# Hybrid attention and expert-retrieval step on one core: experts gathered by pairs of heads from within the query stage, inverse roots by ACT as exponentials of logarithms

## The chip, the cores and the metric

The kernel runs on one core of one Trainium2 chip. The metric is the device time of one execution in microseconds (us), the median of several runs. The engines are called by the names of the profile: PE (matrix engine), DVE (vector engine), ACT (activation engine), POOL (GpSimd, which issues the gathers and half of the cache pages here) and SP (which issues the other transfers). The core has 16 DMA engines.

## The reference, cut to what matters

One layer for 512 prompt tokens and 8 sample tokens, all in float32. Of the parts, these matter here:

```python
def rmsnorm(x, g):
    y = x * lax.rsqrt(jnp.mean(x * x, axis=-1, keepdims=True) + RMS_EPS)
    return y * g

xn = rmsnorm(h, norm1_g); z = xn @ w_in                      # "first" norm
qa = rmsnorm(qa, qa_norm_g); ka = rmsnorm(ka, ka_norm_g)     # "head" norms, 8 heads x 64
ya = sb_attend(qa, (past_k, ka), (past_v, va), ...)          # samples read 32 pages of 128 keys each
ob, s_new = gla_scan(...); yb = rmsnorm(ob, ob_norm_g) * silu(rb)   # "output" norm, 4 heads x 128
h = h + (ga * (ya @ w_up_a) + gb * (yb @ w_up_b)) @ w_o
h = h + peer(rmsnorm(h, norm2_g), w_peer_q, peer_sub_keys, expert_u, expert_v)
h = h + (p @ w_ple) * sigmoid(rmsnorm(h, norm3_g) @ w_ple_gate)

def peer(x, w_q, sub_keys, expert_u, expert_v):
    q = (x @ w_q).reshape(t, 8, 2, 128)                      # 8 heads, 2 halves
    s = einsum('thcd,hcnd->thcn', q, sub_keys)               # 128 scores for each of 16 lists
    s1, i1 = top_k(s[:, :, 0], 16); s2, i2 = top_k(s[:, :, 1], 16)
    top_s, top_c = top_k(s1[..., :, None] + s2[..., None, :], 16)    # per head, of 256 sums
    e = i1[top_c // 16] * 128 + i2[top_c % 16]               # 8 heads x 16 experts a token
    g = softmax(top_s)
    act = gelu(einsum('td,thkd->thk', x, expert_u[e]))
    return einsum('thk,thkd->td', g * act, expert_v[e])
```

Each token so reads 128 experts, and each expert is a row of 1024 values of u and 1024 of v (8 KB).

## The kernel before

The five engines run programs written out by hand; semaphores order them, and nothing reorders them. A single program goes through these stages:

- **Front.** The first norm, the projections (items of PE that ACT takes out of the banks), the head norms, the gated linear attention, and the output norm. For each norm PE makes the mean of squares, ACT its root (`roots`, `ob_root`), and DVE a reciprocal and the products (`head_norm`, `ob_norm`).
- **Samples' cache.** Eight samples read 32 pages of keys and 32 of values each (256 KB a page). POOL issues the key pages into `kring` (8 slots); DVE multiplies and sums them by pairs of pages (`keys`, one pair is one multiplication and one reduction), as filler between its other steps; `HEAD_KEYS` says how many pairs stand in each head of the attention stage. The value pages go into `vring` (8 slots): the first `V_EARLY * PAGES` are issued by SP, the others by POOL, and from sample 5 on they use `kring` too, once the last keys are multiplied. PE multiplies value pages in half rings of four pages (`v_half`), and each sample ends with `own_heads` on DVE, `v_fold` on PE and `take_v` on ACT.
- **Attention stage**, 8 heads; then the **gate stage** of pass 0 (tokens 0 to 255): `gate_tiles`, `up_tiles` on PE, `mix_rows` on DVE, 8 times; then `wo_tiles` (8 times), the second norm, the transposes.
- **Query stage** of pass 0: 16 times `queries(0, j)` and `scores(0, j - 1)` on PE, `take_queries` and `take_scores` on ACT, `key_lists(0, j)` on DVE (the best 16 of 128 scores, for two tiles of 128 tokens). After lists 4, 8, 12 and 15 DVE selects the experts of tile 0 for a pair of heads (`select_pair`), and `select_end` makes the 128 expert numbers and gates of each token at once. Value pages of samples 5 to 7 are multiplied between the queries (`V_IN_PQ`), and the folds stand at `FOLD_PQ`.
- **Gather stage**, 4 tiles of 128 tokens, 32 steps a tile, 128 steps in all. A step works on four of the eight slots of `gring`. POOL issues one indirect DMA for each slot (128 rows of 8 KB, line 654), DVE makes the dot products (line 1519), ACT the gelu, the coefficients and two diagonal matrices (lines 1049 to 1058), PE multiplies (`expert_values`, line 1984) and so frees two slots at a time (`g_used`). Odd slots use lists whose halves are swapped; SP copies these (`other_lists`). `second_pass` puts the whole of pass 1 (gates, wo, queries, 48 weight tiles of 512 KB) and the selection of tiles 1 and 2 between the steps of tiles 0 and 1; `embeddings` puts the final norm and the selection of tile 3 and of the samples between the steps of tiles 2 and 3.
- **Tail**: the last tile's sums, the samples' experts, the final norm and the outputs.

The gather stage waits for all value pages, since `gring` lies over the rings: POOL waits on `v_done` for 8 samples and on `y_taken`, and then on `sel_ready` and `lists_landed` for each tile, which are counted by tile. Weight tiles go through `wring` (3 slots) in the order of `stream` on SP; a tile waits there until PE has used the one three before it. Nearly every operation of DVE and ACT is recorded at line 154, that of the helper `also`, so groups are told apart by operation and size; `L1116` and `L1128` are the sum and the product of `keys`, `L1657` `v_half`, `L1850` and `L1862` gates and ups, `L1878` wo, `L1907` queries, `L1917` scores, `L1668` folds, `L623` pages issued by POOL.

## Time and profile before

| | us |
|---|---|
| median of 3 runs | 2206.96 (2206.49 to 2214.03) |
| the profiled execution | 2213.31 |
| its span, first to last instruction | 2211.6 |
| outside the span | 1.7 |

The page gives the busy time of each engine, the span in 40 slices, the DMA queues and the chain of work that ended last. To place the stages on the time axis, read three instructions: the last page issued by POOL, the first gather, and the last gather. The windows then show how many GB/s were moved in each stage, and the timelines of single engines show which of them was late. "Granted clock" (PEclk) is a share of the full 2.4 GHz. All times are those of the one profiled execution.

### The profile page before, as it was taken

The page shows a single profiled execution, that of the slowest core. Times are in us where ns is not written, and L with a number is a line of the kernel's source. Part 1 is how long each engine was busy: PE and PEld are TensorE (multiplying, and loading weights), DVE is VectorE, ACT ScalarE, POOL GpSimd, SP SyncE. Part 2 cuts the span into 40 slices and gives each one's busy share as a digit, 9 for nine tenths or more (in the row PEclk, how much of TensorE's full clock was granted, in tenths as well). Part 3 has the DMA queues.
Part 4 walks back from the last instruction along what each step waited for, and adds up shares of the span by engine and source line. Part 5 has one row for each costly group of instructions (what it writes and reads, how often), then busy time and mean ns, then how long its engine had stood idle before and what let it go on. Part 6 is the DMA issues. An engine that isn't in the chain of part 4 may idle for free.

```text
span 2211.6 us, 23735 instructions
## 1 busy us (share of the span) xinstructions
PE 1644.4 (74%) x8044; PEld 762.6 (34%) x8044; DVE 1396.0 (63%) x2571; ACT 618.7 (28%) x1772; POOL 792.8 (36%) x911
## 2 busy tenths in 40 slices
PE   7999976999899277776867886455758555765559
PEld 5638622558456133332213443111212111211112
DVE  2697679769438666565455789556766556666442
ACT  2212213531011134443232222223242223232221
POOL 1131123223353234333443344343444444444430
PEclk9999988999999689998988988777888877877779
DMA  4574497879797599999999999999999999999990
GB/s 149 186 269 169 150 367 252 293 272 343 283 332 295 198 420 419 420 420 391 408 398 420 419 414 391 420 417 397 419 421 412 418 421 413 422 421 421 391 421 18
DMA packets 150698, 769.20 MB, mean 348 GB/s; under 512 B 21544, under 2 KB 23048, under 8 KB 82736
## 3 DMA queue, kind: packets, MB, share of 16 engines
q0 software_dynamic: 105632, 645.98, 72.6%
q1 hardware_dynamic: 44944, 121.70, 15.2%
q8 instruction: 63, 1.03, 0.2%
q14 instruction: 59, 0.48, 0.1%
HBM read 759.41 MB, written 5.58 MB: 346 GB/s over the span
## 4 chain that ended last, share of the span: by engine, by line
DMA 41%; PE 34%; DVE 10%; issue 6%; ACT 4%; POOL 4%; SPq 1%; POOLq 0%; DVEq 0%; ACTq 0%
DMA arena<-experts_in,arena 38%; PE bank L1984 8%; PE bank L1575 5%; POOL arena L654 4%; DVE arena L154 4%; PE bank L1626 3%; DVE arena L1519 3%; PE bank L1657 2%; PE bank L1878 2%; PE bank L1907 2%; DMA arena<-cache_v_in 2%; PE bank L1967 2%; DVE arena L1116 2%; DVE arena L1128 2%; ACT arena L154 1%
## 5 line engine op out<-in xcount | busy, mean ns | idle before, releaser
L1984 PE MATMUL bank<-arena 64*64 64x512 f32 x4096 | 652.0, 768 | 487.6 <-ACT arena L1058 476.4
L1519 DVE CUSTOM_DVE_ANT_0 arena<-arena 128x1024 f32<-128x1024 f32 x512 | 622.6, 1227 | 534.4 <-DMA arena<-experts_in,arena 532.0
L654 POOL DMA_INDIRECT arena<-experts_in,arena x512 | 575.7, 1124 | 856.5 <-PE bank L1984 710.7
L1984 PEld LDWEIGHTS bank<-arena 64*64 64x64 f32 x4096 | 160.2, 160 | 938.7 <-ACT arena L1058 699.6
L1049 ACT ACTIVATE arena<-arena 128x2 f32<-128x2 f32 x256 | 52.1, 203 | 932.0 <-DVE arena L1519 931.8
L623 POOL DMA_DIRECT2D arena<-cache_k_in x256 | 137.8, 538 | 418.7 <-DVE arena L1128 346.9
L1128 DVE TENSOR_TENSOR arena<-arena 128x1024 f32<-128x1024 f32 x128 | 156.4, 1223 | 25.9 <-DMA arena<-scratch_q 14.1
L1116 DVE TENSOR_REDUCE arena<-arena 128x16 f32<-128x1024 f32 x128 | 155.0, 1214 | 0.0
L154 ACT ACTIVATE arena<-bank 128x512 f32<-128x512 f32 (+7 forms) x126 | 54.1, 441 | 308.8 <-PE bank L1575 115.5
L1907 PE MATMUL bank<-arena 128*128 128x256 f32 (+1 forms) x512 | 125.5, 398 | 0.8 <-ACT arena L154 0.8
L1575 PE MATMUL bank<-arena 128*128 128x260 f32 x512 | 122.0, 397 | 5.0 <-DVE arena L154 5.0
L1053 ACT ACTIVATE arena<-arena 128x1 f32<-128x1 f32 x512 | 122.8, 286 | 8.4
L1850 PE MATMUL bank<-arena 128*128 128x256 f32 (+1 forms) x512 | 120.9, 392 | 0.0
L154 DVE TENSOR_TENSOR arena<-arena 128x512 f32<-128x512 f32 (+6 forms) x131 | 108.4, 830 | 12.1 <-ACT arena L154 8.4
L154 ACT ACTIVATE arena<-bank,arena 128x512 f32<-128x512 f32 (+3 forms) x134 | 68.4, 551 | 158.7 <-PE bank L1850 73.0
L1907 PEld LDWEIGHTS bank<-arena 128*128 128x128 f32 x512 | 97.6, 196 | 39.6 <-issue 24.4
L1575 PEld LDWEIGHTS bank<-arena 128*128 128x128 f32 x512 | 99.4, 196 | 28.0 <-issue 11.2
L1850 PEld LDWEIGHTS bank<-arena 128*128 128x128 f32 x512 | 97.2, 193 | 33.4 <-issue 18.0
L1657 PE MATMUL bank<-arena 128*8 128x512 f32 x512 | 97.0, 616 | 14.8 <-DMA arena<-cache_v_in 14.7
L154 ACT ACTIVATE arena<-arena 128x260 f32<-128x260 f32 (+11 forms) x98 | 64.1, 677 | 138.4 <-DVE arena L154 84.7
L154 DVE TENSOR_TENSOR arena<-arena,bank 128x512 f32<-128x512 f32 (+3 forms) x74 | 39.3, 568 | 85.8 <-PE bank L1878 25.0
L623 POOL DMA_DIRECT2D arena<-cache_v_in x128 | 68.9, 538 | 68.1 <-PE bank L1657 46.2
(100 smaller groups left out, 1571.8 us busy)
## 6 DMA issues: line engine op xcount, KB each, us to landing
arena<-cache_k_in POOLq DMA_DIRECT2D x256, 256.0 KB, 5.0
arena<-w_stream_in SPq DMA_DIRECT2D x120, 512.0 KB, 6.5
arena<-cache_v_in SPq DMA_DIRECT2D x128, 256.0 KB, 5.9
arena<-cache_v_in POOLq DMA_DIRECT2D x128, 256.0 KB, 5.4
arena<-experts_in,arena POOLq DMA_INDIRECT x520, 12.6
arena<-xT_in SPq DMA_DIRECT2D x2, 1040.0 KB, 6.3
arena<-scratch_q SPq DMA_DIRECT2D x1, 2048.0 KB, 7.2
arena<-x_rows_in SPq DMA_DIRECT2D x2, 1024.0 KB
```

What stands on the lines that cost most here:

```text
L154: op(*args, **kw).then_inc(sem, 1)
L623: pool.dma_start(slot, cache[bass.ds(page, 1)].rearrange("a p n -> (a p) n")).then_inc(landed, 16)
L654: pool.indirect_dma_start(gring[:, s, :], None, A["experts"], bass.IndirectOffsetOnAxis(ap=rows[:, i * RING_G + s:i * RING_G + s + 1], axi ...
L1053: last = A_(coef[:, s:s + 1], gates_of[:, i * 8 + s:i * 8 + s + 1], ACT.Copy, scale=act_g[:, s:s + 1])
L1116: V.tensor_reduce(z4[:, b:b + 1, first:first + 2, :].rearrange("p a c h -> p (a c) h"), prod[:, 2 * (n % 2):2 * (n % 2) + 2].rearrange("p ...
L1128: V.tensor_tensor(prod[:, 2 * (n % 2):2 * (n % 2) + 2], kring[:, 2 * i:2 * i + 2], q, ALU.mult).then_inc(k_mul, 1)
L1519: last = V.tensor_tensor_reduce(gring[:, s, 0:D], gring[:, s, 0:D], x_rows, 1.0, 0.0, ALU.mult, ALU.add, dot[:, s:s + 1])
L1575: last = mm(out, w[:, k], xn[:, k, a:b], start=(k == 0), stop=(k == KD - 1))
L1657: mm(out[at:at + H, :], w4[:, b, PAGES - 1 - g * RING_V - s], slot, start=False, stop=True, skip_group_check=True).then_inc(v_free, 1)
L1850: last = mm(bank[4 + u][:, 0:b - a], w[:, k], xn[:, k, a:b], start=(k == 0), stop=(k == KD - 1))
L1907: last = mm(bank[4 + j % 2][:, 0:b - a], w[:, k], xn2T[p][:, k, 0:b - a], start=(k == 0), stop=(k == KD - 1))
L1984: last = mm(bank[2 * r + c2][out, :], diag[rows, s], gring[rows, s, cols], start=start, stop=True, skip_group_check=True)
```

## The change

**Pairs.** Tile by tile selection becomes selection by pairs of heads. `select_end` works on the 32 experts of a pair, and `softmax_exp`, `soft_in`, `soft_e`, `sel_ready`, `lists_landed` and `other_lists` are counted by pair (four to a tile); the samples keep theirs in one. POOL's gathers of slots 0, 32, 64 and 96 of a tile wait for their own pair.

**Query stage cut.** Ahead of the first gather stand only 10 of the 16 queries of pass 0, 7 of the 16 key lists and pair 0 of tile 0. The other queries, lists and pairs 1 to 3 go between steps 0 and 15 of the gather stage, and pass 1 begins at step 12 (`PASS_AT`), 12 steps later than before. Tables (`QUERIES_AT`, `LISTS_AT`, `PAIRS_AT`, `EMBED_AT`) give the step of each piece.

**Value pages earlier.** SP issues 160 pages in place of 128, the last 32 of them between weight tiles of the gate and wo stages. POOL issues 96, all into the ring of 16 slots. PE's half rings of samples 4 to 7 stand in the gates (4 of them), in wo (14, before 8) and in the first 7 queries (14, before 24). Six pairs of key pages move from the gate stage into the attention stage (`HEAD_KEYS` 36 in sum, before 30; gates 26, before 32).

**Inverse roots.** In the first, head and output norms ACT makes ln(mean + eps) and exp(-0.5 x), in place of a square root on ACT and a reciprocal on DVE. The second and final norms stay.

The memory of the gather stage is laid out in another order, so that the swapped rows (`xsw`) lie where the keys' queries were, and not in a ring.

```diff
-V_EARLY = 4
-V_WIDE = 5 * PAGES
+V_EARLY = 5
+V_FIRST = V_EARLY * PAGES
 V_BANK = (7, 0, 0, 0, 2, 0, 2, 0)
...
-V_IN_PQ = {0: (5, 0), 1: (5, 2), 2: (5, 4), 3: (5, 6), 4: (6, 0), 5: (6, 2), 6: (6, 4), 7: (6, 6),
-           8: (7, 0), 9: (7, 2), 10: (7, 4), 11: (7, 6)}
-V_AFTER = {2: 2, 3: 3, 5: 4, 6: 5, 7: 6}
...
-MASK_PQ = {3: 5, 7: 6, 11: 7}
-FOLD_PQ = {1: 4, 6: 5, 10: 6, 14: 7}
-HEAD_KEYS = (4, 4, 4, 4, 4, 4, 3, 3)
+HEAD_KEYS = (5, 5, 5, 5, 4, 4, 4, 4)
+GATE_KEYS = (4, 4, 3, 3, 3, 3, 3, 3)
+V_IN_GATES = {4: (4, 0), 5: (4, 1), 6: (4, 2), 7: (4, 3)}
+V_IN_WO = {0: ((4, 4),), 1: ((4, 5), (5, 0)), 2: ((4, 6), (5, 1)), 3: ((4, 7), (5, 2)), 4: ((5, 3), (5, 4)),
+           5: ((5, 5), (5, 6)), 6: ((5, 7), (6, 0)), 7: ((6, 1),)}
+V_IN_PQ = {0: (6, 2), 1: (6, 4), 2: (6, 6), 3: (7, 0), 4: (7, 2), 5: (7, 4), 6: (7, 6)}
...
+FIRST_QUERIES, FIRST_LISTS = 10, 7
+QUERIES_AT = ({-1: 9, 0: 10, 1: 11, 3: 12, 4: 13, 5: 14, 6: 15},
+              {g: j for j, g in enumerate((49, 50, 51, 52, 55, 56, 57, 58, 61, 62, 63, 64, 67, 68, 69, 70))})
+LISTS_AT = ({0: 7, 3: 8, 4: 9, 5: 10, 6: 11, 9: 12, 10: 13, 11: 14, 12: 15},
+            {g + 3: j for g, j in QUERIES_AT[1].items()})
+PAIRS_AT = {(0, 1): 1, (0, 2): 7, (0, 3): 13, (1, 0): 17, (1, 1): 23, (1, 2): 29, (1, 3): 35,
+            (2, 0): 56, (2, 1): 62, (2, 2): 68, (2, 3): 74, (3, 0): 78, (3, 1): 82, (3, 2): 86, (3, 3): 90}
+PASS_AT = 12
+EMBED_AT = (76, 92, 108)
+SAMPLE_LISTS_AT = 77
+PAIR_SLOTS = 32
...
-            ("gring", RING_G * 2 * D), ("diag", RING_G * HP), ("xsw", 2 * D), ("expert_sw", 2 * SEL), ("gate_sw", 2 * SEL)])
+            ("xsw", 2 * D), ("expert_sw", 2 * SEL), ("gate_sw", 2 * SEL), ("diag", RING_G * HP), ("gring", RING_G * 2 * D)])
...
+            for m in range(8):
+                stream(gate_use(0, m, 0) + RING_W, gate_use(0, m, 0) + 2 * RING_W)
...
+                elif m == 5:
+                    early_pages(4 * PAGES + RING_V, 4 * PAGES + 2 * RING_V)
+                elif m == 7:
+                    early_pages(4 * PAGES + 2 * RING_V, 4 * PAGES + 3 * RING_V)
+            stream(wo_use(0, 3), wo_use(0, 5))
+            early_pages(4 * PAGES + 3 * RING_V, 5 * PAGES)
+            stream(wo_use(0, 5), pq_use(0, 3))
...
-                sp.wait_ge(sel_ready, t + 1)
+            def other_lists(t, pair):
+                if t // 2 or pair:
+                    sp.wait_ge(lists_landed[t % 2], 64 * (4 * (t // 2) + pair))
+                sp.wait_ge(sel_ready, 4 * t + pair + 1)
+                slots = slice(PAIR_SLOTS * pair, PAIR_SLOTS * pair + PAIR_SLOTS)
                 for to, of in both_halves:
-                    sp.dma_start(expert_sw[to, t % 2], expert[of, t]).then_inc(lists_landed[t % 2], 16)
-                    sp.dma_start(gate_sw[to, t % 2], gate[of, t]).then_inc(lists_landed[t % 2], 16)
-
...
-            sp.wait_ge(v_done, NB)
-            sp.wait_ge(y_taken, 5)
+            sp.wait_ge(k_mul, K_PAIRS + NB * PAGES // 2)
             sp.wait_ge(xn2_ready, 2)
             other_rows(0)
             other_rows(1)
-            other_lists(0)
-
-
-            stream(gate_use(1, 1, 0), wo_use(1, RING_W))
-            other_lists(1)
+            stream(pq_use(0, 3), pq_use(0, 11))
...
-            for i in range(V_EARLY * PAGES // RING_V, NB * PAGES // RING_V):
+            for i in range(V_FIRST // RING_V, NB * PAGES // RING_V):
...
-                    if n < V_WIDE:
-                        pool.wait_ge(v_free, n + 1)
-                    elif n < V_WIDE + RING_K:
+                    if n < V_FIRST + RING_K:
                         pool.wait_ge(k_mul, K_PAIRS + NB * PAGES // 2)
+                    elif n < V_FIRST + 2 * RING_V:
+                        pool.wait_ge(v_free, RING_V + n - 2 * RING_V + 1)
                     else:
-                        pool.wait_ge(v_free, n - 2 * RING_V + RING_V + 1)
+                        pool.wait_ge(v_wide_free, n - V_FIRST - 2 * RING_V + 1)
                     load_page(slot, A["cache_v"], landed, pages[s])
...
-                pool.wait_ge(sel_ready, t + 1)
-                pool.wait_ge(lists_landed[t % 2], 64 * (t // 2 + 1))
                 for i in range(SEL // RING_G):
                     for s in range(RING_G):
+                        pair, slot = divmod(i * RING_G + s, PAIR_SLOTS)
+                        if slot == 0:
+                            pool.wait_ge(sel_ready, 4 * t + pair + 1)
+                        elif slot == 1:
+                            pool.wait_ge(lists_landed[t % 2], 64 * (4 * (t // 2) + pair + 1))
...
+            def inverse_root(out, mean, signal):
+                c.also(A_, out, mean, ACT.Ln, bias=cst("eps"))
+                c.then(A_, out, out, ACT.Exp, scale=-0.5, signal=signal)
+
...
-            c.also(V.reciprocal, rstd, std_row)
...
-                c.then(V.reciprocal, std, std)
...
-                c.then(V.reciprocal, ob_tmp[:, h % 3], ob_tmp[:, h % 3])
...
+            def softmax_exp(t, pair=0):
+                act.wait_ge(soft_in, 4 * t + pair + 1)
+                heads = slice(2 * pair, 2 * pair + 2) if t < NT else slice(0, PH)
+                c.also(A_, top[0:ROWS[t], 1, heads], top[0:ROWS[t], 1, heads], ACT.Exp, signal=soft_e)
...
+            def selection(g):
+
+                for (t, pair), at in PAIRS_AT.items():
+                    if g == at + 1:
+                        softmax_exp(t, pair)
...
+            def select_end(t, heads):
+
+                R, each = ROWS[t], heads.stop - heads.start
+                slots = slice(TOPK * heads.start, TOPK * heads.stop)
                 c.settle()
                 flat = lambda x: x.rearrange("p h k -> p (h k)")
-                c.also(V.scalar_tensor_tensor, out=expert[0:R, t], in0=flat(top[0:R, 7]), scalar=float(NKEYS), in1=flat(top[0:R, 8]),
-                       op0=ALU.mult, op1=ALU.add)
-                dve.wait_ge(soft_e, t + 1)
-                c.also(V.tensor_reduce, den[0:R], top[0:R, 1], AX.X, ALU.add)
-                c.then(V.reciprocal, den[0:R], den[0:R])
-                c.then(V.tensor_tensor, gate[0:R, t].rearrange("p (h k) -> p h k", h=PH), top[0:R, 1],
...
-            for j in range(16):
+            for j in range(4):
                 key_lists(0, j)
-                if j in MASK_PQ:
-                    own_heads(MASK_PQ[j])
-                if j in (4, 8, 12, 15):
-                    pair = (j - 3) // 4 if j < 15 else 3
-                    select_pair(0, pair, False)
-                    select_pair(0, pair, True)
+            select_pair(0, 0, False)
+            own_heads(6)
+            select_pair(0, 0, True)
+            for j in range(4, FIRST_LISTS):
+                key_lists(0, j)
+                if j == 4:
+                    own_heads(7)
...
+                if m in V_IN_GATES:
+                    v_half(*V_IN_GATES[m])
...
+                for b, half in V_IN_WO[i]:
+                    v_half(b, half)
-            for j in range(16):
+            for j in range(FIRST_QUERIES):
...
+                for p in range(2):
+                    if g in QUERIES_AT[p]:
+                        queries(p, QUERIES_AT[p][g])
+                    if g - 1 in QUERIES_AT[p]:
+                        scores(p, QUERIES_AT[p][g - 1])```

**Where instructions stand.** PE at the end of the query stage, before. `L1907` is a query, `L1917` scores, `L1668` a fold, `L1850` a gate tile of pass 1, `L1984` the products of gathered experts:

```order
L1907 MATMUL bank<-arena 128x256 x8
L1917 MATMUL bank<-arena 128x128 x2
L1668 MATMUL bank<-arena 128x1 x4
L1907 MATMUL bank<-arena 128x256 x8
L1917 MATMUL bank<-arena 128x128 x2
L1907 MATMUL bank<-arena 128x256 x8
L1917 MATMUL bank<-arena 128x128 x4
L1850 MATMUL bank<-arena 128x264 x8
L1984 MATMUL bank<-arena 64x512 x16
```

The same place after (`L1958` query, `L1968` scores, `L1719` the last fold, `L2039` the products):

```order
L1719 MATMUL bank<-arena 128x1 x4
L1958 MATMUL bank<-arena 128x256 x8
L1968 MATMUL bank<-arena 128x128 x2
L1958 MATMUL bank<-arena 128x256 x8
L1968 MATMUL bank<-arena 128x128 x2
L1958 MATMUL bank<-arena 128x256 x8
L1968 MATMUL bank<-arena 128x128 x2
L2039 MATMUL bank<-arena 64x512 x16
L1958 MATMUL bank<-arena 128x256 x8
L1968 MATMUL bank<-arena 128x128 x2
L2039 MATMUL bank<-arena 64x512 x16
```

The last fold stands ahead of queries 8 and 9 and of query 10, the first of the six that share the stream with the gather stage; before, all 16 stood ahead of the first products.

DVE at the start of the gather stage, before: the last sums of the last pair, `select_end` over 128 experts, and the first dot product (`L1519`):

```order
L154 TENSOR_TENSOR arena<-arena 128x512 x2
L154 TENSOR_REDUCE arena<-arena 128x32
L154 SCALAR_TENSOR_TENSOR arena<-arena 128x128
L154 TENSOR_REDUCE arena<-arena 128x8
L154 RECIPROCAL arena<-arena 128x8
L154 TENSOR_TENSOR arena<-arena 128x128
L1519 ISA arena<-arena 128x1024
```

DVE after, from the last dot product of step 0 (`L1570`) to the first of step 1:

```order
L1570 ISA arena<-arena 128x1024
L1570 ISA arena 128x1
L169 TENSOR_TENSOR arena<-arena 128x512
L169 MAX arena<-arena 128x8 x2
L169 MAX_INDEX arena<-arena 128x8 x2
L169 MATCH_REPLACE arena<-arena 128x256 x2
L169 MAX arena<-arena 128x8 x2
L169 MAX_INDEX arena<-arena 128x8 x2
L1570 ISA arena<-arena 128x1024
```

The first half of pair 1 now stands ahead of the dot products of step 1; its second half, with a `select_end` over 32 experts, stands ahead of those of step 2.

SP from the weight tiles of the query stage on, before. `L483` is a weight tile, `L532` the swapped rows, `L537` and `L538` the swapped lists:

```order
L483 DMA arena<-w_stream_in 128x1024 x45
L532 DMA arena<-arena 64x1024 x4
L537 DMA arena<-arena 64x128
L538 DMA arena<-arena 64x128
L537 DMA arena<-arena 64x128
L538 DMA arena<-arena 64x128
L483 DMA arena<-w_stream_in 128x1024 x24
```

And after (`L497`, `L554`, `L562`, `L563`):

```order
L497 DMA arena<-w_stream_in 128x1024 x6
L554 DMA arena<-arena 64x1024 x4
L497 DMA arena<-w_stream_in 128x1024 x8
L562 DMA arena<-arena 64x32
L563 DMA arena<-arena 64x32
L562 DMA arena<-arena 64x32
L563 DMA arena<-arena 64x32
L497 DMA arena<-w_stream_in 128x1024 x4
```

The lists of a pair are copied between weight tiles, and SP waits for the pair there.

## Rows read from the trace of the kernel before

**Rows 1.** The page: GB/s in 40 slices of 55.3 us, and the chain by engine.
```profile
GB/s 149 186 269 169 150 367 252 293 272 343 283 332 295 198 420 419 420 420 391 408 398 420 419 414 391 420 417 397 419 421 412 418 421 413 422 421 421 391 421 18
...
DMA 41%; PE 34%; DVE 10%; issue 6%; ACT 4%; POOL 4%; SPq 1%; POOLq 0%; DVEq 0%; ACTq 0%
```

**Rows 2.** POOL, timeline (start, us; idle before, releaser): last pages, first gathers.
```profile
690.86 4.68 POOL L623 DMA_DIRECT2D arena<-cache_v_in  x8 [1.96 <-PE bank L1657]
750.58 1.01 POOL L654 DMA_INDIRECT arena<-experts_in,arena  x1 [55.03 <-DMA arena<-arena]
```

**Rows 3.** Windows, tiles 0, 3, tail: PE, PEld, DVE, ACT, POOL busy, clock, DMA, GB/s.
```profile
750.60:1111.90 361.30, 266.81 (x1428) 118.43 (x1428) 198.40 (x363) 129.24 (x357) 143.69 (x128) 0.90 1.00 411
...
1799.60:2125.60 326.00, 196.21 (x1072) 50.72 (x1072) 197.76 (x355) 92.68 (x334) 144.69 (x128) 0.77 1.01 415
2125.60:2211.60 86.00, 66.34 (x192) 19.37 (x192) 28.70 (x47) 18.80 (x47) 10.91 (x10) 0.86 0.39 162
```

**Rows 4.** Windows of 50 us: end of the query stage, and DVE's densest gather window.
```profile
650.00:700.00 50.00, 49.47 (x274) 30.75 (x273) 36.35 (x154) 5.75 (x16) 30.13 (x56) 1.00 1.01 374
700.00:750.00 50.00, 24.91 (x132) 19.83 (x130) 42.33 (x177) 6.13 (x15) 0.00 (x0) 0.80 0.27 86
1300.00:1350.00 50.00, 41.48 (x260) 21.99 (x258) 43.81 (x144) 14.90 (x60) 19.14 (x18) 0.93 1.01 410
```

**Rows 5.** Windows, DVE alone: a key list, a pair, `select_end`.
```profile
634.10:637.20 3.10, 2.84 (x16) 1.00 0.98 373
661.80:672.10 10.30, 9.79 (x30) 1.00 1.01 375
744.80:745.95 1.15, 0.99 (x5) 0.50 0.00 0
```

**Rows 6.** PE, timeline: gate stage's end, wo tiles, queries, value half rings between.
```profile
571.19 6.29 PE L1878 MATMUL bank<-arena 128*128 128x512 f32 x8 [5.64 <-DVE arena L154]
...
612.31 1.05 PE L1657 MATMUL bank<-arena 128*8 128x512 f32 x8
...
620.22 5.68 PE L1907 MATMUL bank<-arena 128*128 128x256 f32 x16 [0.78 <-ACT arena L154]
...
629.46 3.72 PE L1907 MATMUL bank<-arena 128*128 128x256 f32 x16
633.01 0.61 PE L1917 MATMUL bank<-arena 128*128 128x128 f32 x4
633.55 1.91 PE L1657 MATMUL bank<-arena 128*8 128x512 f32 x16
```

**Rows 7.** POOL, timeline: value pages, eight after eight.
```profile
650.85 4.69 POOL L623 DMA_DIRECT2D arena<-cache_v_in  x8 [1.93 <-issue]
657.46 4.68 POOL L623 DMA_DIRECT2D arena<-cache_v_in  x8 [1.92 <-issue]
```

**Rows 8.** DMA issues of the page: a value page, KB, us to landing.
```profile
arena<-cache_v_in POOLq DMA_DIRECT2D x128, 256.0 KB, 5.4
```

**Rows 9.** DVE's reciprocals as a group, 0 to 340 us; ACT's second root.
```profile
L154 DVE RECIPROCAL arena<-arena 128x520 f32<-128x520 f32 x13 | 44.2, 3401 | 65.5 <-ACT arena L154 65.3
21.20 0.48 ACT L154 ACTIVATE arena<-bank,arena 128x260 f32<-128x260 f32 x1 [1.68 <-PE bank L1548]
```

**Rows 10.** DVE: the keys' product on the page; two waits in the attention stage.
```profile
L1128 DVE TENSOR_TENSOR arena<-arena 128x1024 f32<-128x1024 f32 x128 | 156.4, 1223 | 25.9 <-DMA arena<-scratch_q 14.1
...
426.09 0.69 DVE L154 TENSOR_TENSOR arena<-bank,arena 128x512 f32<-128x512 f32 x1 [8.37 <-PE bank L1657]
458.80 1.49 DVE L154 TENSOR_TENSOR arena<-arena 128x1280 f32<-128x1280 f32 x1 [2.51 <-ACT arena L154]
```

**Rows 11.** Waits, 750 to 2150 us, and a table load of ACT with its successor.
```profile
ACT arena L1049 <- DVE arena L1519: 931.8, 247, 11.1
...
1003.19 1.28 ACT L154 ACT_TABLE_LOAD   x1
1004.48 0.48 ACT L154 ACTIVATE arena<-bank,arena 128x264 f32<-128x264 f32 x1
```

307 lines of the change are left out of this document (156 added, 151 removed).

## Prediction

> **What bounds the kernel now.** I read the GB/s of the page first [rows 1]. There are two kernels in it. In slices 0 to 13 the rate moves between 149 and 367 GB/s and no engine is full throughout. From slice 14 on it stands at 391 to 422 GB/s until the tail. The chain of waits agrees: 41% of it is DMA. The border is found on POOL: the last value pages are issued at 690.9 us, and the first gather only at 750.6, after 55 us of idle [rows 2]. The windows by tile show what the gather stage is made of [rows 3]. A tile gathers 128 times 128 rows of 8 KB, 134.2 MB, which takes 323 us at the 415 GB/s of tile 3; tile 3 took 326. Tile 0 took 361 at 411 GB/s, because weights of pass 1 go by too: 32 tiles of 0.524 MB are 41 us at that rate, and 320 + 41 = 361 (tile 1 is the same to a microsecond, with the other weights). So the stage lasts as long as its bytes need, and whatever starts it earlier moves the end, unless it brings bytes with it or breaks the rate.
>
> Why does it start at 750.6? In the window 650 to 700 PE is busy for 49.5 of 50 us and the DMA for all of it; in 700 to 750 PE for 24.9, DVE for 42.3, and the DMA moves 86 GB/s [rows 4]. DVE is the last one there: it works off key lists and pairs until `select_end` at 744.8 to 745.9 [rows 5], and the copies of the lists and POOL follow by 750.6.
>
> **The part ahead of the first gather.** Two conditions are cut: all 16 lists and 4 pairs become 7 lists and 1 pair, and the value pages, which PE finished with the queries, are spread forward. I follow PE from the wo stage, where it starts at 571.2 after waiting 5.6 us for DVE [rows 6].
>
> *Up to the wo stage.* The first norm loses a reciprocal of 3.4 us on the path (13 of them stand up to 340 us, 44.2 us of DVE [rows 9]); ACT's second root takes 0.48 us and is followed by one more such operation, so -3 us. The four head norms of queries and the four of keys lie beside a full PE: nothing. The output norms save 13.6 us of DVE, but slice 5 moves 367 GB/s [rows 1], as much as pages ever get, so the pages and not DVE set much of that pace: between 0 and -10, I take -4. In the attention stage six more pairs of keys, a product of 1.22 us and a sum of about the same, are 15 us of DVE; the two waits shown there hold 10.9 us [rows 10], so +4. In the gate stage four half rings and one opening product on PE cost +5, and DVE, with six pairs fewer, no longer keeps PE waiting 5.6: -0.6. Sum: -3.6, between -13 and +6.
>
> *The wo stage.* Before, 8 half rings of 1.05 us stand in it, and the last ends at 613.4; the queries start at 620.2 [rows 6]. Now there are 14, with one opening product and the fold of sample 4: 8 us of PE. Besides, pages come later than PE wants them. POOL issues eight pages in 6.61 us when nothing holds it [rows 7], while PE would take eight in 3.7 + 2 x 1.05 = 5.8 us, and pages 168 to 175 are only issued once PE has used pages of sample 4 in the third and fourth wo tiles; each then needs 5.4 us to land [rows 8]. I count waits of 2, 3 and 2 us: +7. Queries start at 620.2 + 15 = 635, and +8 would be the least.
>
> *The query stage.* A query with scores and two half rings is 3.7 + 0.6 + 1.9 = 6.2 us less overlap, 5.95 from start to start [rows 6]; the first takes 5.7 alone; a fold or an opening product adds 1. Queries 0 to 6 (two folds, one opening) end at 635 + 5.7 + 1.9 + 6 x 5.95 + 3 = 681.5; query 7 without pages at 686; the fold of sample 7, query 8, and ACT's copy: 693. DVE gets there at the same time: list 3 can start after query 4 at 668, then one list 3.1, a pair 10.3 and its end 1.15 with ACT's exponential [rows 5], 684; three lists more, 9.3, with `own_heads(7)` of 0.7: 694. Before, DVE had 9 lists and 3 pairs more. POOL's pages from 168 on, 88 of them, go out from about 592 (571.2 + three tiles 13.7 + four half rings 4.2 + 3 of other products) and need 11 x 6.61 us, until 665: ahead of PE's need, so no bound in this stage. With the -3.6 the first gather falls at **690**, between 675 and 715, in place of 750.6: -60.
>
> **The gather stage.** Six query tiles of 0.524 MB move behind the start: 3.1 MB at 411 GB/s, +7.5 us. All other bytes are the same. Nine lists (3.1) and three pairs (10.3 + 1.15) move into steps 0 to 14: 62 us of DVE. A step is 10.2 us of DMA in tile 3 and 11.3 in tile 0, 15 steps are some 160 us; their dot products take 15 x 4 x 1.24 = 74. So DVE would be busy for 136 of 160, 85%. The trace has such a place: 1300 to 1350 us, DVE 43.8 of 50, 88%, at 410 GB/s [rows 4]. There the ring takes it, so I take +1 for it; the lists of pass 1 and tile 2 are spread wider than before, which may give that back. Pairs 1 to 3 are ready at steps 2, 8 and 14, and the first gathers that need them belong to steps 8, 16 and 24, issued two steps ahead: hidden by at least 4 steps. Twelve more exponentials bring 24 table loads of 1.28 us, 31 us of ACT, beside 129 busy of 361 [rows 3]: ACT waits for DVE for 932 us of the stage [rows 11]: +1, between 0 and +31.
>
> A rule speaks against this edit. The trace shows a table load of 1.28 us with the next operation 0.01 us behind it [rows 11]. The Trainium skill, ScalarE: Activation LUTs, What ACT_TABLE_LOAD costs, adds a drain of 1.38 us to each switch, 2.66 in all; by it the 24 loads would be 64 us of ACT, and the estimate for the worst case 33 us worse than by the row. The row shows no drain, and the sum goes by the row.
>
> **The tail** of 86 us [rows 3] is untouched.
>
> **Sum.** -60 + 7.5 + 1 + 1 = -50.5. The profiled execution (2213.31, span 2211.6) would become 2162.8, its span 2161. It lies 6.35 us above the median of 2206.96; taken from that, the median after is **2156**.
>
> **Rivals.**
> *A, the pages are late.* The SP queue now interleaves pages and weights in order, and the wo stage wants 8 pages and a tile, 2.6 MB, in 5.8 us, 450 GB/s, where 374 were the most shown for pages. If each of its waits doubles and the query stage inherits them, the gather starts at 705 to 730: median 2171 to 2196. For it: DMA is full in 650 to 700. Against: what is moved forward leaves that window.
> *B, DVE's work is exposed in the ring.* In a step the list or the half pair stands ahead of the dot products. The slots of that step are freed only after ACT and PE have followed, and if the DMA runs dry meanwhile, the work is paid in full: +62, and with ACT's table loads +31 more. Then the sum is -60 + 7.5 + 62 = +9.5, median 2216, up to 2247. It turns slower once more than 52 of the 62 us are exposed, that is if nearly every piece stops the DMA. For it: ACT's long wait on DVE, and that half of the ring is only 10 us of DMA. Against: the window at 88%. Half exposed gives 2185.
> *C, the front is better still.* Output norms pay in full and pages come in time: start at 677, median 2143, down to 2138.
> *D, the pair lists do not let the gather go early*, because SP reaches `other_lists(0, 0)` only after the tile of query 10 was issued, which waits for query 7 at 686. That is 5 us ahead of my start; if it decided, the start would be 695 and the median 2161. It lies inside the forecast.
>
> **Chances.** The forecast with D, 2146 to 2170: 0.62. C and better: 0.12. A, and B in part, 2171 to 2194: 0.17. Within 0.5% of before (about what a measurement of this kernel can tell from no change, 2196 to 2218): 0.05, B nearly whole. Slower by more: 0.04, B with ACT. The range for 8 in 10 runs from 2134 to 2184, the bounds of the start and a part of A. Faster 0.91, same 0.05, slower 0.04.
>
> **What would show it.** POOL's first gather at about 690, after the key lists and not after an idle of 55 us. Wo stage with waits of PE for value pages, queries from about 631. A gather stage (first to last gather) of 1375 + 7.5 + 2 = 1384 us. GB/s of 400 or more in the first 150 us of it, with DVE at 40 to 45 of 50. No reciprocals of 3.4 us. I am wrong if the start is later than 715, or if windows of the first 15 steps fall below 390 GB/s.

## The result, and the profile after

The changed kernel takes 2186.96 us (2183.36 to 2190.53, 4 runs) beside 2207.08 for the kernel before on the same chip: a ratio of 0.9913, interval 0.9896 to 0.993. It is faster, by 20 us. I had forecast 2156, with 2134 to 2184 as the range, so the gain is 31 us short and the time lies 3 us outside. The profiled execution took 2187.64, its span 2186.0; before it was 2211.6.

The page of the changed kernel, GB/s in 40 slices of 54.7 us:

```profile
span 2186.0 us, 23971 instructions
...
GB/s 151 207 270 155 145 367 253 329 354 303 280 334 229 413 413 417 416 419 415 407 364 416 399 420 420 418 410 419 417 391 401 406 419 421 416 419 410 384 422 28
```

Against [rows 1] the plateau over 400 begins a slice earlier, in slice 13; its deepest dip is 364, in slice 20. POOL's timeline answers to [rows 2]; columns are start, duration, engine, line, operation, and in brackets the idle time ahead and what ended it:

```profile
706.84 1.01 POOL L697 DMA_INDIRECT arena<-experts_in,arena  x1 [26.60 <-ACT arena L169]
708.15 0.97 POOL L697 DMA_INDIRECT arena<-experts_in,arena  x1 [0.30 <-issue]
```

The first gather starts at 706.8, 44 us earlier and not 60. The rest of the loss is behind it. The DMA from the first gather to the last but one of the 512, of the kernel before and then of the changed one (packets, MB; the queue of the gathers, q0, and SP's, q1; the share is that of 16 engines in the stretch):

```profile
DMA packets 83705, 567.35 MB, mean 413 GB/s; under 512 B 10140, under 2 KB 11196, under 8 KB 18188
...
q0 software_dynamic: 73041, 531.96, 94.0%
q1 hardware_dynamic: 10592, 34.47, 6.4%
...
arena<-w_stream_in SPq DMA_DIRECT2D x44, 512.0 KB, 7.9
```

```profile
DMA packets 88658, 571.34 MB, mean 410 GB/s; under 512 B 14871, under 2 KB 15159, under 8 KB 23185
...
q0 software_dynamic: 72987, 531.56, 93.1%
q1 hardware_dynamic: 15594, 38.81, 7.3%
...
arena<-w_stream_in SPq DMA_DIRECT2D x52, 512.0 KB
```

Eight weight tiles more, 4.2 MB, and 410 in place of 413 GB/s.

The span cuts into stretches that can be read in every trace: the first gate tile, the first wo tile, the first query, the first gather, and the transposes of the last tile, which end the gather stage. All in us:

| kernel | gates start | to wo | to queries | to first gather | to last transposes | median |
|---|---|---|---|---|---|---|
| before | 479.7 | 91.5 | 49.0 | 130.4 | 1402.4 | 2207 |
| forecast | 476.7 | 90.9 | 63.8 | 58.6 | 1411.9 | 2156 |
| changed | 473.6 | 99.3 | 66.2 | 67.7 | 1420.9 | 2187.0 |
| own6 | 474.2 | 98.0 | 64.5 | 60.4 | 1419.6 | 2175.7 |
| exp5 | 469.6 | 98.3 | 65.6 | 67.0 | 1417.7 | 2181.7 |
| both | 470.9 | 99.8 | 66.2 | 59.7 | 1421.0 | 2177.9 |
| norms | 468.8 | 91.7 | 48.1 | 131.9 | 1399.5 | 2202.1 |
| gates | 475.6 | 97.1 | 66.0 | 64.9 | 1418.9 | 2185.4 |
| pair13 | 478.2 | 96.5 | 64.0 | 66.5 | 1419.4 | 2184.1 |
| more | 476.5 | 97.4 | 64.2 | 66.9 | 1447.2 | 2213.5 |
| early | 469.6 | 97.1 | 63.5 | 54.6 | 1422.4 | 2172.3 |
| split | 476.5 | 92.3 | 65.3 | 66.8 | 1420.4 | 2179.9 |
| mix7 | 470.9 | 95.1 | 67.7 | 68.0 | 1420.3 | 2180.5 |
| lists2 | 479.4 | 97.6 | 65.5 | 67.7 | 1421.9 | 2184.8 |
| best2 | 474.3 | 91.4 | 66.8 | 53.4 | 1419.2 | 2168.3 |
| keys30 | 466.3 | 102.0 | 65.4 | 67.6 | 1417.7 | 2186.4 |
| whole | 468.1 | 97.1 | 65.5 | 125.9 | 1409.0 | 2231.7 |
| spaced | 474.2 | 98.1 | 64.1 | 66.4 | 1428.4 | 2189.1 |
| best3 | 471.2 | 92.1 | 64.8 | 53.8 | 1428.9 | 2170.4 |
| pieces | 469.2 | 97.4 | 65.6 | 64.6 | 1419.4 | 2180.7 |

The forecast's row is made from the prediction's own terms. Kernels that share a stretch show how far one profile can be trusted there: the start of the gates lies between 468.1 and 479.4 in the 16 kernels with the changed kernel's front (mean 473.3), gates to wo between 95.1 and 99.8, the query stage between 64.6 and 68.0, the gather stage between 1417.7 and 1421.0 where its code is the same. A difference of one profile below 3 us in a late stretch says nothing, then. The intervals of the medians are some 3 to 6 us wide to each side, so one median against another means little below 5 us, and the stretches tell more. The kernel before, measured again beside each set of experiments, had medians of 2204.4 to 2208.0.

### The profile page after: what moved, and what is told of

Read it like the earlier page. It is cut to its first block, busy times and chain, and to the rows that moved or that the text cites. A ratio compares the mean times of both kernels' runs of the same rounds, so it can differ in the third digit from the quotient of the medians.

```text
span 2186.0 us, 23971 instructions
## 1 busy us (share of the span) xinstructions
PE 1645.4 (75%) x8044; PEld 768.0 (35%) x8044; DVE 1365.8 (62%) x2670; ACT 655.6 (30%) x1830; POOL 769.2 (35%) x879
## 3 DMA queue, kind: packets, MB, share of 16 engines
q8 instruction: 63, 1.03, 0.2%
## 4 chain that ended last, share of the span: by engine, by line
DMA 39%; PE 38%; DVE 9%; issue 5%; ACT 4%; POOL 4%; SPq 1%; POOLq 0%; DVEq 0%; ACTq 0%
DMA arena<-experts_in,arena 36%; PE bank L2039 9%; PE bank L1626 5%; DVE arena L169 4%; POOL arena L697 4%; DVE arena L1570 4%; PE bank L1677 3%; DMA arena<-cache_v_in 2%; PE bank L1901 2%; PE bank L1708 2%; PE bank L2022 2%; PE bank L1958 2%; PE bank L1929 2%; PE bank L1913 1%; ACT arena L169 1%
## 5 line engine op out<-in xcount | busy, mean ns | idle before, releaser
L2039 PE MATMUL bank<-arena 64*64 64x512 f32 x4096 | 636.8, 752 | 441.8 <-ACT arena L1108 415.2
L1570 DVE CUSTOM_DVE_ANT_0 arena<-arena 128x1024 f32<-128x1024 f32 x512 | 622.1, 1226 | 477.0 <-DMA arena<-experts_in,arena 467.1
L697 POOL DMA_INDIRECT arena<-experts_in,arena x512 | 570.9, 1115 | 852.0 <-PE bank L2039 733.5
L2039 PEld LDWEIGHTS bank<-arena 64*64 64x64 f32 x4096 | 157.4, 157 | 866.4 <-ACT arena L1108 608.0
L1174 DVE TENSOR_TENSOR arena<-arena 128x1024 f32<-128x1024 f32 x128 | 156.4, 1223 | 28.8 <-DMA arena<-scratch_q 16.7
L169 ACT ACTIVATE arena<-bank 128x512 f32<-128x512 f32 (+7 forms) x126 | 53.9, 439 | 304.4 <-PE bank L1626 106.1
L1958 PE MATMUL bank<-arena 128*128 128x256 f32 (+1 forms) x512 | 131.9, 413 | 6.4 <-DVE arena L169 5.6
L1901 PE MATMUL bank<-arena 128*128 128x256 f32 (+1 forms) x512 | 122.4, 395 | 4.5 <-DMA arena<-w_stream_in 4.5
L169 ACT ACTIVATE arena<-bank,arena 128x512 f32<-128x512 f32 (+3 forms) x134 | 69.0, 550 | 174.3 <-PE bank L1901 79.7
L1958 PEld LDWEIGHTS bank<-arena 128*128 128x128 f32 x512 | 102.4, 206 | 49.5 <-issue 26.2
L169 DVE TENSOR_TENSOR arena<-arena 128x512 f32<-128x512 f32 (+6 forms) x169 | 114.4, 679 | 5.9 <-ACT arena L169 1.8
L1708 PE MATMUL bank<-arena 128*8 128x512 f32 x512 | 100.1, 616 | 16.7 <-DMA arena<-cache_v_in 16.5
L1901 PEld LDWEIGHTS bank<-arena 128*128 128x128 f32 x512 | 98.0, 195 | 38.8 <-issue 17.6
L169 ACT ACTIVATE arena<-arena 128x260 f32<-128x260 f32 (+9 forms) x136 | 77.5, 586 | 104.4 <-DVE arena L169 51.9
L169 DVE TENSOR_TENSOR arena<-arena,bank 128x512 f32<-128x512 f32 (+3 forms) x74 | 39.4, 569 | 109.0 <-PE bank L1929 29.3
L169 DVE SCALAR_TENSOR_TENSOR arena<-arena 128x520 f32<-128x520 f32 (+6 forms) x52 | 34.8, 680 | 102.3 <-ACT arena L169 101.2
## 6 DMA issues: line engine op xcount, KB each, us to landing
arena<-cache_k_in POOLq DMA_DIRECT2D x256, 256.0 KB, 4.8
arena<-w_stream_in SPq DMA_DIRECT2D x120, 512.0 KB
arena<-cache_v_in SPq DMA_DIRECT2D x160, 256.0 KB, 5.5
arena<-cache_v_in POOLq DMA_DIRECT2D x96, 256.0 KB, 5.4
```

The lines of the kernel that those rows point to most:

```text
L169: op(*args, **kw).then_inc(sem, 1)
L697: pool.indirect_dma_start(gring[:, s, :], None, A["experts"], bass.IndirectOffsetOnAxis(ap=rows[:, i * RING_G + s:i * RING_G + s + 1], axi ...
L1174: V.tensor_tensor(prod[:, 2 * (n % 2):2 * (n % 2) + 2], kring[:, 2 * i:2 * i + 2], q, ALU.mult).then_inc(k_mul, 1)
L1570: last = V.tensor_tensor_reduce(gring[:, s, 0:D], gring[:, s, 0:D], x_rows, 1.0, 0.0, ALU.mult, ALU.add, dot[:, s:s + 1])
L1708: mm(out[at:at + H, :], w4[:, b, PAGES - 1 - g * RING_V - s], slot, start=False, stop=True, skip_group_check=True).then_inc(v_free if b < ...
L1901: last = mm(bank[4 + u][:, 0:b - a], w[:, k], xn[:, k, a:b], start=(k == 0), stop=(k == KD - 1))
```

## The experiments

Each edit is to the changed kernel, unless said otherwise.

### Who holds the first gather: PE's fold or the exponential

In the changed kernel three engines wait for each other at the end of the query stage. PE, around the fold of sample 6 (L1719); L1958 is a query, L1968 scores, L1708 half rings:

```profile
670.04 2.43 PE L1708 MATMUL bank<-arena 128*8 128x512 f32 x16
679.26 1.87 PE L1719 MATMUL bank<-arena 128*128 128x1 f32 x8 [6.79 <-DVE arena L169]
680.99 6.64 PE L1958 MATMUL bank<-arena 128*128 128x256 f32 x16
687.48 0.61 PE L1968 MATMUL bank<-arena 128*128 128x128 f32 x4
```

DVE, the same time: first half of pair 0 from 673.58, `own_heads(6)` at 678.54, second half, and the wait for the exponential:

```profile
673.58 0.69 DVE L169 TENSOR_TENSOR arena<-arena 128x512 f32<-128x512 f32 x1
...
678.54 0.67 DVE L169 TENSOR_TENSOR arena<-bank,arena 128x512 f32<-128x512 f32 x1
...
696.03 0.18 DVE L169 TENSOR_REDUCE arena<-arena 128x2 f32<-128x32 f32 x1 [11.44 <-ACT arena L169]
```

ACT: it takes the fold, query 5 and query 6, and only then makes the exponential:

```profile
681.17 0.18 ACT L169 ACTIVATE arena<-bank 128x4 f32<-128x4 f32 x1 [10.63 <-PE bank L1719]
687.67 0.38 ACT L169 ACTIVATE arena<-bank 128x256 f32<-128x256 f32 x1 [6.33 <-PE bank L1958]
...
694.47 1.28 ACT L169 ACT_TABLE_LOAD   x1
695.77 0.23 ACT L169 ACTIVATE arena<-arena 128x32 f32<-128x32 f32 x1
```

The longer wait is DVE's 11.44 us. Which of the two sets the start? `own6` takes away the first, `exp5` the second, `both` both.

```diff
             for j in range(4):
+                if j == 3:
+                    own_heads(6)
                 key_lists(0, j)
             select_pair(0, 0, False)
-            own_heads(6)
             select_pair(0, 0, True)
```

> Edit to the changed kernel: DVE masks sample 6 (own_heads(6)) ahead of key list 3 and no longer between the halves of pair 0. Theory (PE's fold of sample 6 stands behind DVE's first half of the pair, and everything after it on PE is late by that): PE's wait of 6.79 us at 679.26 is gone, the query behind it takes 3.7 and not 6.64 us, and the first gather moves from 706.8 to about 697 (-9.5); DVE's wait for the exponential shrinks by the same since ACT follows PE. The median falls from 2187 to about 2178. Rival (the exponential's place on ACT holds the start, not the fold): first gather within 2 us of 706.8, median within 2 us of 2187.

Median 2175.68, ratio 0.9868 (0.9852 to 0.9885). PE and POOL of `own6`:

```profile
668.62 2.82 PE L1709 MATMUL bank<-arena 128*8 128x512 f32 x16
671.37 1.05 PE L1720 MATMUL bank<-arena 128*128 128x1 f32 x8
672.28 3.71 PE L1959 MATMUL bank<-arena 128*128 128x256 f32 x16
```

```profile
697.16 1.01 POOL L697 DMA_INDIRECT arena<-experts_in,arena  x1 [18.56 <-ACT arena L169]
```

No wait, and the query behind it runs in 3.71 us. DVE's wait shrank to 2.21 us without being touched. The first gather is at 697.16, where 697 was expected.

```diff
-                if j == 6:
+                if j == 5:
                     softmax_exp(0, 0)
```

> Edit to the changed kernel: ACT makes the exponential of pair 0 after query 5 and not after query 6. Theory (PE is the path and DVE's wait of 11.44 us lies beside it): DVE's wait falls to about 6 us, since ACT's query 5 is itself late by PE's fold, but the first gather moves by under 1 us, from 706.8 to about 706.4; median within 2 us of 2187. Rival (the exponential holds the start): first gather at about 701, median 2181.

Median 2181.66, ratio 0.99 (0.9883 to 0.9916). DVE's wait fell to 5.47 us, and from first query to first gather it is 67.0 us in place of 67.7. The first gather stands at 700.3, the rival's number, but the whole front of this execution is 5 us earlier: the queries began at 633.4 and not at 639.2. The median, 2181.66, is the rival's number too, but its interval and the changed kernel's overlap. The stretch decides, for the theory, and `both` agrees.

> Edit to the changed kernel: both moves, own_heads(6) ahead of list 3 and the exponential after query 5. Theory: no wait of PE for the fold and none of DVE over 1.5 us for the exponential; PE's queries alone set the start, so the first gather is at about 696 to 697, as with the first move alone, and the median about 2177 to 2178. Rival (each of the two waits was a part of it): about 691, median 2172, and then it must lie more than 4 us below the kernel with the first move alone.

Median 2177.89, ratio 0.9874 (0.9857 to 0.989), first gather at 696.51, stretch 59.7: the second move adds 0.7 us to the first. The fold's wait was the path, and the longest wait of the region was its shadow.

### What the inverse roots alone are worth

`norms` is the kernel before with the inverse roots of the change alone (here the head norms; first and output norms alike):

```diff
-                    c.also(A_, norm_buffers(j)[1][:, a:b], bank[6 + half][:, 0:HALF], ACT.Sqrt, bias=cst("eps"), signal=qkstd)
+                    inverse_root(norm_buffers(j)[1][:, a:b], bank[6 + half][:, 0:HALF], qkstd)
...
-                c.then(V.reciprocal, std, std)
```

> The kernel before with the inverse roots alone: ACT makes logarithm and exponential in the first, head and output norms, DVE's 13 reciprocals of 3.4 us are gone, and nothing else is changed. The theory of the prediction: -3 in the first norm and -4 in the output norms, nothing in the head norms, so the gates begin at about 472.5 in place of 479.7 and the median falls from 2207 to about 2200. Rival (pages and not DVE set the pace up to the gates): -3 alone, gates at 476.7, median 2204. Rival on the other side (two operations and more table loads on ACT stand ahead of PE): gates later than 479.7.

Median 2202.10 against 2205.64, ratio 0.9986 (0.9972 to 1.0): 3.5 us, at the rival's -3. The profile shows the gates at 468.8, 10.8 us ahead of the kernel before. That is the trap of one profile: the kernel before was profiled in an execution 6.35 us above its median. From the gates on the two profiles differ by little over 1 us, so the front is the likely place of those 6 us; one pair of profiles can't show more. 10.8 less 6.3 is 4.5.

### The gate stage, 8 us too long

The changed kernel's PE and SP there (L1901 and L1913 are gates and ups, L515 value pages and L497 weight tiles):

```profile
553.36 1.05 PE L1708 MATMUL bank<-arena 128*8 128x512 f32 x8
557.92 10.21 PE L1901 MATMUL bank<-arena 128*128 128x256 f32 x32 [3.51 <-DMA arena<-w_stream_in]
```

```profile
544.12 4.48 SPq L515 DMA_DIRECT2D arena<-cache_v_in  x8
548.66 23.28 SPq L497 DMA_DIRECT2D arena<-w_stream_in  x6
```

PE waits 3.51 us for the tile behind the eight pages, and then takes 10.21 us for two gate tiles that cost 7.18 otherwise. The window around it, the one ahead of it, and parts of it (the wait lies in 554 to 558):

```profile
543.62:553.62 10.00, 10.00 (x50) 8.38 (x52) 6.64 (x7) 0.95 (x2) 2.14 (x4) 1.00 0.92 311
553.62:563.62 10.00, 6.49 (x21) 4.55 (x14) 9.13 (x10) 0.00 (x0) 2.02 (x4) 0.68 0.60 222
...
554.00:556.00 2.00, 0.41 (x4) 0.00 (x0) 1.97 (x4) 0.00 (x0) 0.00 (x0) 1.00 1.07 415
556.00:558.00 2.00, 0.08 (x1) 0.08 (x1) 1.87 (x2) 0.00 (x0) 0.00 (x0) 0.81 1.02 406
558.00:560.00 2.00, 2.00 (x5) 1.64 (x6) 1.87 (x3) 0.00 (x0) 0.00 (x0) 0.50 0.29 115
560.00:562.00 2.00, 2.00 (x6) 1.55 (x6) 2.00 (x3) 0.00 (x0) 0.54 (x1) 0.50 0.00 0
```

Over the 10 us the DMA's share is 0.60, but while PE waits it is full, at 406 to 415 GB/s, and right behind the wait it is idle. So the bytes are not too many for the stage; the eight pages, 2.1 MB or 5 us at that rate, pass ahead of a tile that PE wants first. Is SP, besides, held by the pages' slots?

```diff
-V_IN_GATES = {4: (4, 0), 5: (4, 1), 6: (4, 2), 7: (4, 3)}
+V_IN_GATES = {4: ((4, 0), (4, 1)), 6: ((4, 2),), 7: ((4, 3),)}
...
```

> Edit to the changed kernel: both first half rings of sample 4 stand behind gate tile 4 on PE, so that SP's eight value pages in the middle of the gate stage find their slots free when SP reaches them and hold no weight tile. Theory (the gate stage is 8.4 us longer than forecast because SP's pages stand ahead of weight tiles): PE's wait of 3.51 us for a weight tile at 557.9 and the slower tile behind it are gone; from the first gate to the first wo tile 92 to 94 us in place of 99.3; the median -5. Rival (the DMA itself is full there, pages and weights together): the wait only moves, and the stretch stays at 98 to 100.

Median 2185.42, ratio 0.9923 (0.9897 to 0.9949). The wait is 4.06 us at 559.1, the stretch 97.1, no less than in kernels without the edit: the theory fails. SP had not waited for slots: eight issues take 4.15 us by themselves. The next edit keeps the pages and takes them apart; the first weight tile of gate 7 goes ahead of them, and two of the four half rings stand behind gate 4, two behind gate 7.

```diff
-V_IN_GATES = {4: (4, 0), 5: (4, 1), 6: (4, 2), 7: (4, 3)}
+V_IN_GATES = {4: ((4, 0), (4, 1)), 7: ((4, 2), (4, 3))}
...
+                if m == 6:
+                    for u in range(3):
+                        stream(gate_use(0, m, 0) + RING_W + u, gate_use(0, m, 0) + RING_W + u + 1)
+                        first = 4 * PAGES + RING_V
+                        early_pages(first + 3 * u, min(first + 3 * u + 3, first + RING_V))
...
-                elif m == 5:
-                    early_pages(4 * PAGES + RING_V, 4 * PAGES + 2 * RING_V)
```

> Edit to the changed kernel: the eight value pages that SP issues together in the gate stage (136 to 143, 4.5 us of issuing, 2 MB) go in threes behind single weight tiles, the first weight tile of gate 7 ahead of them; their two half rings stand behind gate 7. Theory (the wait is neither for free slots, which the earlier edit gave without effect, nor for a full DMA, whose share is 0.83 to 0.92 there, but for the eight pages in a row ahead of one tile): PE's wait of 3.5 us at 557.9 goes, and the gate stage takes 92 to 94 us in place of 97 to 99. Rival (the wait only moves to the next tile, since the same bytes pass in the same time): 96.5 to 99.5 us again, with a wait of PE for a weight or a page elsewhere in the stage or at the start of wo.

Median 2179.92, ratio 0.9877 (0.9858 to 0.9895), the stretch 92.3. PE and SP of `split`:

```profile
555.09 3.62 PE L1907 MATMUL bank<-arena 128*128 128x256 f32 x16
559.83 3.72 PE L1907 MATMUL bank<-arena 128*128 128x256 f32 x16 [1.12 <-DMA arena<-w_stream_in]
```

```profile
550.58 1.39 SPq L517 DMA_DIRECT2D arena<-cache_v_in  x3
552.02 0.43 SPq L497 DMA_DIRECT2D arena<-w_stream_in  x1
552.64 1.46 SPq L517 DMA_DIRECT2D arena<-cache_v_in  x3
```

The same bytes, with a wait of 1.12 us in place of 3.51 and at full pace behind it: the cost was the order, eight pages ahead of one tile, with a ring of three tiles behind. How much of it was their issuing (4.15 us) and how much their transfer (5 us) no run tells apart.

```diff
-HEAD_KEYS = (5, 5, 5, 5, 4, 4, 4, 4)
-GATE_KEYS = (4, 4, 3, 3, 3, 3, 3, 3)
+HEAD_KEYS = (4, 4, 4, 4, 4, 4, 3, 3)
+GATE_KEYS = (4, 4, 4, 4, 4, 4, 4, 4)
```

> Edit to the changed kernel: key pages are multiplied in the order of before, 30 pairs in the attention stage and 32 in the gate stage, in place of 36 and 26. Theory of the prediction (six pairs cost the attention stage 4 us and save PE a wait of 5.6 us for DVE ahead of wo): the gates begin some 4 us earlier, at 466 to 474, and gates to wo takes 4 to 6 us longer, 102 to 104; median within 2 us of the changed kernel's. Rival (the gate stage is held by weights and pages, not by DVE): 97 to 99.5 again, and the median falls by 2 to 4.

Median 2186.44, ratio 0.9907 (0.9886 to 0.9927). Gates start at 466.3, 7 us ahead of the mean of the others, and the gate stage takes 102.0, the longest of all: one pays the other, as the theory had it. But PE's wait there, 6.87 us, ends with a weight tile and not with DVE.

### The gather stage: DVE's work, holes, packets

`more` gives DVE six more products of 128x512 in each of the first 15 steps, which nobody reads.

```diff
                 for step in range(STEPS):
+                    if t == 0 and step < 15:
...
+                        for n in range(6):
+                            c.then(V.tensor_tensor, onehot[:, 0:2], every, every, ALU.is_equal)
...
                     pass_work(t * STEPS + step)
```

> Edit to the changed kernel: in each of the first 15 steps of the gather stage DVE makes six more products of 128x512 that nobody reads, 4.3 us a step and 64 us in all, as much again as the lists and pairs that the change moved there. Theory of the prediction (DVE's work lies beside the DMA there): the first 250 us still run at 400 GB/s or more, and the stretch from first gather to last transposes grows by under 8 us. Rival B of the prediction (DVE's work is exposed): it grows by the 64 us, or by half of them. In between: DVE is at about 70% of the early windows now and would be near 100%, so what goes over is paid; by the windows that is 10 to 20 us.

Median 2213.48, ratio 1.004 (1.0026 to 1.0054), slower than before; the stretch grew by 26.3 us, above the 10 to 20 us of the expectation in between and below the half of the rival. Windows of the changed kernel and of `more` from the first gather on (PE, PEld, DVE, ACT and POOL busy with instructions, clock, DMA share, GB/s):

```profile
757.00:807.00 50.00, 35.25 (x208) 17.21 (x208) 37.53 (x111) 15.10 (x55) 20.69 (x19) 0.90 1.01 420
807.00:857.00 50.00, 29.22 (x179) 9.74 (x180) 39.80 (x122) 16.38 (x54) 21.05 (x21) 0.83 1.00 409
```

```profile
757.00:807.00 50.00, 34.94 (x208) 18.90 (x207) 48.05 (x125) 12.11 (x47) 17.47 (x18) 0.93 0.97 385
807.00:857.00 50.00, 20.90 (x120) 6.14 (x124) 48.12 (x114) 13.19 (x44) 14.05 (x15) 0.73 0.83 327
```

With the 62 us that the change moved there DVE is busy for 37.5 to 39.8 of 50 and the DMA full. With 64 more it is at 48 of 50, and 41% of them are paid. So the first 62 were hidden but for a few us (`whole`, below, bounds them), and there was room for some 38 of the next 64.

The changed kernel's worst hole is where wo of pass 1 begins: PE waits 12.23 us for DVE, and at 1135 to 1145 the DMA is idle for half the time:

```profile
1130.00:1135.00 5.00, 2.75 (x4) 1.22 (x5) 3.37 (x8) 1.27 (x5) 0.00 (x0) 0.50 1.03 400
1135.00:1140.00 5.00, 5.00 (x10) 1.43 (x8) 2.55 (x5) 1.27 (x5) 0.00 (x0) 0.75 0.43 174
1140.00:1145.00 5.00, 5.00 (x36) 1.76 (x36) 1.13 (x2) 1.27 (x5) 1.87 (x2) 1.00 0.47 133
```

The first suspect is the pair selected in the same step. `pair13`, in `PAIRS_AT`:

```diff
-(1, 3): 35,
+(1, 3): 32,
```

> Edit to the changed kernel: pair 3 of tile 1 is selected in steps 32 and 33 and not in 35 and 36, where PE waits 12.23 us for DVE behind it. Theory (DVE's half pair ahead of what PE waits for runs the ring dry there): the DMA idle of 5.4 us some 430 us after the first gather is gone, the round of 40.3 us takes 34 to 36, and from the first gather to the last tile's transposes 1416 us in place of 1420.9. Rival (PE's wait is that of the kernel before, which has a round of 36.3 us at its wo tiles): the hole stays within 1 us of what it is and the stretch within 1.5 us of 1420.9.

Median 2184.11, ratio 0.9903 (0.9883 to 0.9924). The hole stays, 4.0 us of idle DMA, and the stretch is 1419.4: the rival. PE asks for the eighth mix at step 36, and DVE makes it at the start of step 37, behind dot products that wait for slots that PE has not freed.

```diff
-                if step % 3 == 1 and 4 <= step <= 25:
+                if step % 3 == 1 and 4 <= step <= 22:
                     mix_rows(1, step // 3 - 1)
+                elif step == 24:
+                    mix_rows(1, 7)
```

> Edit to the changed kernel: DVE mixes the last block of pass 1 at the start of step 36, where PE asks for it, and not at the start of step 37. Theory (PE waits 12.23 us for it with the products of step 36 behind it, the slots are not freed, and the ring runs dry; the kernel before has the same hole at its step 24): the DMA idle of 5.4 us at 430 us after the first gather is gone, the round of 40.3 us takes under 30, and from first gather to last transposes 1415 to 1416 us in place of 1420.9. Rival (DVE's second half of pair 3 in the same step makes the hole): DVE is late with the mix anyway, and at least half of the idle stays.

Median 2180.50, ratio 0.9883 (0.9866 to 0.99). The hole is gone. `mix7` in two windows of the place (its front is 5 us earlier):

```profile
1130.00:1135.00 5.00, 5.00 (x16) 1.49 (x18) 1.73 (x4) 1.27 (x5) 2.24 (x2) 1.00 1.01 418
1135.00:1140.00 5.00, 3.63 (x32) 0.95 (x32) 2.47 (x4) 1.27 (x5) 2.52 (x2) 1.00 1.02 424
```

Round 20 of eight gathers is reached 446.6 us after the first gather, 5 to 8 us sooner than in the changed kernel and its like (451.7 to 454.3). At the last transposes nothing of it is left: 1420.3. The mechanism is right and the expected gain is not there; that it comes back in the next 40 rounds is seen, why is not.

`lists2` halves the copies of the swapped lists (eight of 64 B packets for a pair in place of four of 128 B):

```diff
-                slots = slice(PAIR_SLOTS * pair, PAIR_SLOTS * pair + PAIR_SLOTS)
-                for to, of in both_halves:
...
+                for first in (PAIR_SLOTS * pair, PAIR_SLOTS * pair + PAIR_SLOTS // 2):
+                    slots = slice(first, first + PAIR_SLOTS // 2)
+                    for to, of in both_halves:
...
```

> Edit to the changed kernel: each swapped list goes in two halves of 16 slots, so twice as many copies (8 a pair) and packets of half the size; the bytes are the same. Theory (the DMA moves 410 and not 413 GB/s from first to last gather because the lists go in packets of 128 B): the 60 more copies cost about as much as the change's 48 more did, 3 to 6 us, in the stretch from first gather to last transposes, 1424 to 1427 us. Rival (the rate is lost in holes, not in packets): within 1.5 us of 1420.9.

Median 2184.80, ratio 0.9895 (0.9876 to 0.9914), stretch 1421.9: the rival, by 4825 more packets and 1.0 us, which is inside the scatter of 3 us. Small packets are no great part of it.

`whole` puts all 16 queries, 16 lists and 4 pairs of tile 0 ahead of the first gather again, and keeps the rest.

```diff
-FIRST_QUERIES, FIRST_LISTS = 10, 7
-QUERIES_AT = ({-1: 9, 0: 10, 1: 11, 3: 12, 4: 13, 5: 14, 6: 15},
+FIRST_QUERIES, FIRST_LISTS = 16, 16
+QUERIES_AT = ({},
...
                 if j == 4:
                     own_heads(7)
+                if j % 4 == 3:
+                    select_pair(0, j // 4, False)
+                    select_pair(0, j // 4, True)
```

> Edit to the changed kernel: all 16 queries, 16 lists and 4 pairs of tile 0 stand ahead of the first gather again; earlier value pages, lists and ends by pair, and pass 1 from step 12 stay. Theory (the stretch from first gather to last transposes is 19 us longer than before because eight weight tiles, 10 us, and the work of 9 lists and 3 pairs went into it): 1403 to 1406 us, and from first query to first gather 108 to 115 in place of 67.7, by DVE's 16 lists of 3.1 and 4 pairs of 11.4 us; median 2207 to 2214, so that the spreading is what makes the change a gain. Rival (the later start of pass 1 and the smaller, more frequent lists of all tiles cost the 9 us): 1410 to 1413 us in the stretch.

Median 2231.68, ratio 1.0113 (1.0091 to 1.0135). The query stage takes 125.9 us, more than expected: DVE works through 16 lists and 4 pairs with a wait of 10.2 us for the first exponential. The median, too, lies 18 us above what was expected. The gather stage takes 1409.0, between theory (1403 to 1406) and rival (1410 to 1413). It moves 45 weight tiles and 567.95 MB, beside 52 and 571.34 in the changed kernel and 44 and 567.35 before. Of the 18.5 us by which the changed kernel's stretch exceeds that of before, 11.9 are gone with the spread work, 8.3 of them for 3.39 MB at 410 GB/s. The other 6.6 remain, and 0.6 MB more than before is only 1.5 of them. They lie late: from round 40 to the samples' round, the last, `before` and `norms` need 489.7 and 489.5 us, `whole` 495.0, the changed kernel 496.6, and every kernel with the change between 493 and 498.5. The bytes of these rounds are the same, 202.5 to 203.4 MB, at 415 GB/s before and 409 in the other two.

Two more kernels looked for these. In steps 90 and 91, where both halves of a pair and an embedding stand side by side, DVE is busy nearly without a gap from 1722.5 to 1747.7. `spaced` pulls them apart:

```diff
-                    if g == at + 1:
+                    if g == at + 2:
                         softmax_exp(t, pair)
...
-                    if g in (at, at + 1):
-                        select_pair(t, pair, g == at + 1)
+                    if g in (at, at + 2):
+                        select_pair(t, pair, g == at + 2)
...
-            (2, 0): 56, (2, 1): 62, (2, 2): 68, (2, 3): 74, (3, 0): 78, (3, 1): 82, (3, 2): 86, (3, 3): 90}
+            (2, 0): 56, (2, 1): 62, (2, 2): 68, (2, 3): 74, (3, 0): 79, (3, 1): 83, (3, 2): 87, (3, 3): 92}
```

> Edit to the changed kernel: the two halves of every pair stand two steps apart, not one, and the pairs of tile 3 at steps 79, 83, 87 and 92, so that none shares a step with the embedding of step 90. Theory (DVE's selection in lumps of two neighbouring steps, 4.3 and 5.6 us ahead of dot products, empties the ring some 0.5 us at a time, where 11 small pieces a tile did not): from first gather to last transposes 1412 to 1416 us in place of 1420.9, and the dips of the last 490 us, where DMA moves under 380 GB/s for 5 us, fall from 12 to 6 or fewer. Rival (the rate is lost for another reason): within 1.5 us of 1420.9, with as many dips.

Median 2189.07, ratio 0.9926 (0.9903 to 0.9949), and the stretch is 7.5 us longer, which neither theory nor rival had. A pair half now shares step 64, the border of a tile, with `residual`, for which PE waits 10.50 us:

```profile
1445.00:1450.00 5.00, 5.00 (x12) 3.87 (x13) 4.83 (x21) 1.27 (x5) 0.00 (x0) 0.50 0.88 337
1450.00:1455.00 5.00, 5.00 (x40) 2.69 (x42) 5.00 (x10) 2.37 (x10) 0.43 (x1) 0.91 0.36 119
1455.00:1460.00 5.00, 5.00 (x50) 1.84 (x42) 2.40 (x15) 1.52 (x6) 3.31 (x4) 1.00 0.75 251
```

The hole, 5 us of idle DMA, stands between rounds 20 and 40, and so does the loss: 0.4 us at round 20, over 7 at round 40. That it alone is the cause is not shown, since the edit moves every pair. `pieces` changes tile 3's selection alone, into the kernel before's 11 pieces over all heads (`PIECES_AT` gives their steps):

```diff
+PIECES_AT = {g: n for n, g in enumerate((76, 78, 79, 81, 82, 84, 85, 87, 88, 89, 91))}
...
+                elif n == 5:
+                    select_places(3, ALL, soft_in)
...
+                elif n == 10:
+                    select_end(3, ALL)
```

> Edit to the changed kernel: the selection of tile 3 alone is cut again into 11 pieces over all heads, in steps 76 to 91, with one exponential, in place of four pairs of two halves in steps 78 to 91; the DVE work is the same. Theory (lumps of DVE there lower the rate): the last 24 rounds, from round 40 on, take 489 to 492 us in place of 496.6 (the kernel before: 489.7), with 6 to 8 places of 5 us under 380 GB/s in place of 12, and first gather to last transposes 1414 to 1416. Rival (the lumps are as harmless as the ring was for the first 15 steps): within 2 us of 496.6 and 1420.9.

Median 2180.72, ratio 0.9896 (0.9871 to 0.9921). The last 24 rounds take 496.2, the stretch 1419.4: the rival, and in tile 3 the lumps are not the cause.

### The combinations

`early` has the first move of `own6`, ACT's copy of the samples' columns ahead of query 8, and DVE's release of the ring behind `own_heads(7)`:

```diff
                 if j == 4:
                     own_heads(7)
+                    dve.sem_inc(g_used, 4)
...
-            dve.sem_inc(g_used, 4)
...
+                if j == 8:
+                    c.settle()
+                    c.also(A_, yaT[:, :, SEQ:T], v_cols, ACT.Copy, signal=y_taken)
                 take_queries(0, j)
...
-                elif j == 8:
-                    c.settle()
-                    c.also(A_, yaT[:, :, SEQ:T], v_cols, ACT.Copy, signal=y_taken)
```

> Edit to the changed kernel: own_heads(6) ahead of list 3 as before; ACT copies the samples' columns ahead of query 8 and not behind it, and DVE frees the ring behind own_heads(7), not behind list 6. Theory (with the fold's wait gone, the start is held by the copy at 696.1 and by DVE's list 6 at 695.2, neither of which the first gather needs; the swapped lists land at about 693): from the first query to the first gather 56 to 57 us, in place of 60.4 with the first move alone and 67.7 in the changed kernel; median 2172 to 2175. Rival (the start is worth nothing by then because PE is not at the products until query 10 is done): the first gather is earlier, but the stretch from it to the last transposes is longer by as much.

Median 2172.31, ratio 0.9866 (0.9836 to 0.9896); query stage 54.6, gather stage 1422.4. Of the 5.8 us gained over `own6`, 2.8 come back in the gather stage. POOL's second gather needs the swapped lists and waits 3.92 us for them, which would account for it:

```profile
684.77 1.01 POOL L697 DMA_INDIRECT arena<-experts_in,arena  x1 [15.22 <-ACT arena L169]
689.70 0.97 POOL L697 DMA_INDIRECT arena<-experts_in,arena  x1 [3.92 <-DMA arena<-arena]
```

`best2` is `early`, `split` and `mix7` in one.

> All that may help in one kernel: own_heads(6) ahead of list 3, the samples' copy and the release of the ring early, the pages in the gate stage between single weight tiles, and the last mix a step earlier. Theory (each part acts in its own stretch): gate stage 92 to 94, query stage to first gather 54 to 56, first gather to last transposes 1415 to 1417 us; median 2163 to 2167. Rival (what is gained ahead is given back in the ring): 2171 to 2174, the median of the kernel with the early release alone.

Median 2168.32 (2165.78 to 2168.95), ratio 0.9828 (0.9814 to 0.9841), against 0.9913 (0.9896 to 0.993) for the changed kernel: the fastest, about 19 us ahead of it. The gate and query stages gave what was expected (91.4 and 53.4), the gather stage 1419.2 and not 1415 to 1417. `best3` adds the spacing of `spaced` to it.

> The best kernel so far with the halves of the pairs two steps apart and tile 3's pairs off the embedding's step. Theory: gate stage and query stage as there (91 to 93, 53 to 55), the stretch from first gather to last transposes 1411 to 1415 in place of 1419.2, median 2161 to 2165 in place of 2168.3. Rival: 2167 to 2170.

Median 2170.37, ratio 0.9837 (0.9816 to 0.9858): gates and queries as in `best2`, and the gather stage as in `spaced`, 1428.9. Its median, no lower than that of `best2`, misses the theory's 2161 to 2165.

## Where the prediction was right, and the steps that failed

In the order of its sum. The stretches miss by -3.1, +8.4, +2.4, +9.1 and +9.0 us, 25.8 in all, and the span by 24.9. The largest single step that failed is the overlap of PE and DVE in the query stage: PE's fold of sample 6 waits 6.79 us for a DVE step inside pair 0, and without that wait the stretch is 60.4 us in place of 67.7 (`own6`).

**Up to the gates: the number agrees by luck.** I had -3 for the first norm, -4 for the output norms, +4 for six key pairs. The -3.1 by which the changed kernel beats my row is owed to the pair of executions (see the profile and the median, below), and one profile scatters by 11 us here. `norms` gives -3.5 by the medians for all norms, in place of my -7, and `keys30` confirms the exchange between attention and gate stage. Together that leaves about nothing of the -3 in my sum. Probably the pages and not DVE set the output norms' pace, so my -4 was near 0; no run has that norm alone.

**The gate stage: failed, 8 us.** The step is "four half rings and one opening product on PE cost +5 ... DVE ... no longer keeps PE waiting 5.6: -0.6". The work was counted, and the wait for DVE did go (0.37 us is left). What I left out is what those half rings need: eight pages on SP's queue and in the DMA ahead of a weight tile, for which PE waits 3.51 us and then runs 3.03 us slower. Rival A said this for the wo stage and I looked for it only there. `split` gets 5 us of it back.

**The wo stage: right.** Three waits for pages of 1.03, 2.00 and 0.42 us stand there, 3.5 in all in place of 7; but two half rings that take 1.91 us elsewhere took 3.89, and one and a half 3.13, while their pages came in. 66.2 us against 63.8.

**The query stage: failed, 9 us, the largest single step.** I followed PE ("Queries 0 to 6 ... end at ... 681.5") and DVE ("DVE gets there at the same time: ... 684") side by side, gave a fold 1 us, and never crossed the two lines. Fold 6 stands ahead of query 5, about 671, and needs `own_heads(6)`, which the diff puts in the middle of pair 0. With `own6` the stretch is 60.4 against my 58.6.

**The bytes: right in kind, short in size.** Six query tiles gave +7.5; it was eight tiles and, at my rate, 10.2. I counted the queries that stand behind the first gather in the program, not the tiles that PE had used by then. Before, PE had used the 16 query tiles and the first gate tile of pass 1, with three more on their way; in the changed kernel it had used nine and was at query 9. The lists in SP's order did not hold the tiles: SP was past them at 702.4, and the next tile went out at 705.0, when query 8 had ended.

**DVE's work in the ring: right.** +1 for 62 us. `whole` leaves 3.6 us for it beside the bytes, about the scatter, and `more` shows that I was not far from the edge: of the next 64 us 26 are paid. Rival B, with 62 exposed, is refuted, and so is its ACT half: the 24 more table loads are there (78 against 54, each 1.28 us), and the ring of the first steps kept its rate. The rule that I weighed, the Trainium skill, ScalarE: Activation LUTs, What ACT_TABLE_LOAD costs, gives an estimate of 64 us for them; the row of ACT above has the exponential 0.02 us behind its load, with no drain between.

**The other tiles: failed, 6.6 us in `whole`.** "The lists of pass 1 and tile 2 are spread wider than before, which may give that back": the sign was wrong. `whole` has 6.6 us more than before, 1.5 of them for bytes, and 5.3 us of the 6.6 stand in the last 24 rounds, whose bytes are equal. The lumps of two halves in tile 3 (`pieces`), the packets (`lists2`) and the pair beside wo (`pair13`) are not it, and filling the hole (`mix7`) does not shorten the stage. The cause stays open. Not tried are the later embeddings and the new places of ring and swapped rows in memory.

**The tail: right**, 58.3 us behind the last transposes, before 58.7.

**Profile and median: why 31 and not 25.** I took off the 6.35 us by which before's profiled execution lies above its median. For the median that was right. But the forecast's row above is worked out from that execution, and the changed kernel's profile lies only 0.7 above its median, so the row flatters me by 5.7 us. If those stand in before's front, as `norms` suggests, my terms up to the gates missed by 2.6 us where the row shows 3.1 to the good.

**The rivals.** D was inside the forecast and did not decide: SP reached the lists at 699.95, and the first gather at 706.84 waited for ACT's copy behind query 8. In `early`, where that copy comes sooner, the lists do hold the second gather. A was right in mechanism, in another stage. 0.17 of the chance stood at 2171 to 2194, which is where it ended, by several causes of which each was small: the place was foreseen, not the reason.

**A sum of the prediction.** "320 + 41 = 361" for tile 0 does not come out of its own numbers: 134.2 MB at 411 GB/s are 327 us, and the window holds 30 weight tiles and not 32 (148.5 MB in all). The forecast uses only the rate, so nothing follows.

## What to carry to other kernels

When an order is rewritten by hand, write down for each engine's step what it needs of the others, and at what time: every coupling inside a phase, not only the last condition of the phase. The longest wait in a region can be the shadow of a shorter one ahead of it; take them away one at a time. Transfers that go with moved work pass ahead of what stands behind them in the queue, even where the stage as a whole has bandwidth to spare; here a prefetch ring of three tiles did not cover a row of eight pages.

A profile is one execution. Compare stretches between landmarks, over several kernels that share them, before a difference of 5 us is explained.

## What the runs showed of the hardware

Taking a hole of 5 us out of a stream that otherwise runs at 420 GB/s did not shorten it (`mix7`), while a new one of the same size at the tile's border, with a smaller one behind it, went with 7.5 us more (`spaced`, which moves other work too). 4825 more packets, lists in packets of 64 B in place of 128 B, at the same bytes, went with 1.0 us of 1420, inside the scatter (`lists2`). A DMA issue costs SP's queue 0.52 us a page, so eight of them are 4.15 us in which nothing else of that queue starts. And PE ran two gate tiles in 10.21 us behind a wait of 3.51 and in 7.18 without one, so this wait cost nearly twice its length. PE had been busy throughout the window ahead, at a granted clock of 1.00; it fell to 0.81 in the last 2 us of the wait and to 0.50, which is 1.2 GHz, right behind it. The loss behind a wait does not grow with it: after 4.06 us the same two tiles took 8.86 (`gates`), after 6.87 us 9.26 (`keys30`).
